# A third seven-product step in the last half of a macaron block's second down stages

## The reference, cut to what matters

```python
def swiglu(h, wg, wu, wd):
    return (jax.nn.silu(h @ wg) * (h @ wu)) @ wd
...
x = x + 0.5 * swiglu(rmsnorm(x, ffn1_norm[i]), ffn1_wg[i], ffn1_wu[i], ffn1_wd[i])
x = x + hybrid_mixer(rmsnorm(x, mix_norm[i]), ...)
x = x + 0.5 * swiglu(rmsnorm(x, ffn2_norm[i]), ffn2_wg[i], ffn2_wu[i], ffn2_wd[i])
return rmsnorm(x, final_norm)
```

## Time and profile before

| | |
|---|---|
| median of 3 runs | 1812.29 us (1810.42 to 1814.05) |
| profiled execution | 1811.32 us, span of its instructions 1809.5 us |
| TensorE matmul busy | 1796.6 us, 99% of the span, 8109 instructions |
| VectorE busy | 1555.6 us, 86% |
| ScalarE busy | 1069.5 us, 59% |
| DMA | 386.20 MB, mean 213 GB/s |

### The profile page before, as it was taken

The page is one execution under the profiler, slowest core; times in us unless marked ns, Lnnn a source line. Parts: engine busy times, 40 slices in busy tenths (PEclk is TensorE's granted clock), DMA queues, the critical chain, the costliest instruction groups (busy, mean ns, idle before and its releaser), DMA issues.

```text
span 1809.5 us, 22149 instructions
## 1 busy us (share of the span) xinstructions
PE 1796.6 (99%) x8109; PEld 1476.4 (82%) x8110; DVE 1555.6 (86%) x1913; ACT 1069.5 (59%) x1424; POOL 309.2 (17%) x514
## 2 busy tenths in 40 slices
PE   9999999999999999999999999999999999999998
PEld 7778888888888888888788888888888888888886
DVE  7989998889999997679567867899999879999997
ACT  6656655555666566556577745566665455666554
POOL 1122221002222100000122300122221000332100
PEclk9999999999999999999999999999999999999999
DMA  7778887678888667766544655678886677888764
GB/s 244 209 222 234 246 243 219 198 218 237 236 239 245 209 201 215 210 202 201 151 133 117 209 175 175 210 230 237 242 238 216 203 222 224 240 238 252 239 202 159
DMA packets 209661, 386.20 MB, mean 213 GB/s; under 512 B 20164, under 2 KB 25008, under 8 KB 209424
## 3 DMA queue, kind: packets, MB, share of 16 engines
q1 hardware_dynamic: 185008, 352.37, 62.5%
q0 software_dynamic: 22016, 30.90, 8.2%
q10 hardware_dynamic: 2528, 1.52, 0.3%
HBM read 368.98 MB, written 4.19 MB: 206 GB/s over the span
## 4 chain that ended last, share of the span: by engine, by line
PE 87%; DVE 7%; DMA 3%; ACT 1%; issue 1%; ACTq 0%; DVEq 0%; SPq 0%
PE ps L829 18%; PE ps L831 18%; PE ps L830 18%; PE ps L847 7%; PE ps L849 7%; PE ps L848 7%; PE ps L817 3%; PE ps L809 3%; PE ps L811 3%; DVE w_lo L1899 2%; DMA raw<-in_ffn_wg_dram 2%; PE ps L896 2%; DVE wt_lo L1971 1%; DMA w_lo<-in_ffn_wg_dram 1%; DVE wt L1961 1%
## 5 line engine op out<-in xcount | busy, mean ns | idle before, releaser
L1899 DVE TENSOR_TENSOR w_lo<-raw,w_hi 128x1024 fp32r<-128x1024 f32 (+1 forms) x565 | 645.0, 1159 | 108.5 <-ACT w_hi L1379 104.3
L1379 ACT ACTIVATE w_hi<-raw 128x1024 fp32r<-128x1024 f32 x565 | 587.9, 1054 | 203.5 <-PE ps L831 109.0
L829 PE MATMUL ps<-w_hi,hT_hi 128*128 128x512 f32 x972 | 381.7, 393 | 1.4 <-ACT gu L1473 1.2
L831 PE MATMUL ps<-w_hi,hT_lo 128*128 128x512 f32 x972 | 378.9, 390 | 0.0
L830 PE MATMUL ps<-w_lo,hT_hi 128*128 128x512 f32 x972 | 378.6, 390 | 0.0
L1430 ACT ACTIVATE wt_hi<-wt 128x1024 fp32r<-128x1024 f32 x180 | 189.7, 1054 | 289.4 <-DVE wt L1961 289.4
L737 POOL DMA_DIRECT2D gu_raw<-gu_sq x352 | 188.4, 544 | 362.4 <-DVE gu_sq L2146 352.5
L1971 DVE TENSOR_TENSOR wt_lo<-wt,wt_hi 128x1024 fp32r<-128x1024 f32 x180 | 219.3, 1218 | 0.0
L829 PEld LDWEIGHTS ps<-w_hi,hT_hi 128*128 128x128 f32 x972 | 182.6, 188 | 39.1 <-ACT gu L1473 1.6
L831 PEld LDWEIGHTS ps<-w_hi,hT_lo 128*128 128x128 f32 x972 | 182.4, 188 | 38.8
L830 PEld LDWEIGHTS ps<-w_lo,hT_hi 128*128 128x128 f32 x972 | 182.6, 188 | 36.6
(11 more groups left out here) (319 smaller groups left out, 2824.9 us busy)
## 6 DMA issues: line engine op xcount, KB each, us to landing
raw<-in_ffn_wu_dram SPq DMA_DIRECT2D x176, 512.0 KB, 5.0
raw<-in_ffn_wd_dram SPq DMA_DIRECT2D x176, 512.0 KB, 4.8
raw<-in_ffn_wg_dram SPq DMA_DIRECT2D x175, 512.0 KB, 4.7
raw<-in_w_in_dram SPq DMA_DIRECT2D x88, 512.0 KB, 3.7
w_lo<-in_ffn_wg_dram POOLq DMA_DIRECT2D x72, 256.0 KB, 6.7
raw<-in_w_out_dram SPq DMA_DIRECT2D x32, 512.0 KB, 4.2
gu_raw<-gu_sq POOLq DMA_DIRECT2D x352, 32.0 KB, 3.6
x_parked<-x SPq DMA_DIRECT2D x8, 256.0 KB, 5.3
```

Of the source, the lines that this page charges most:

```text
L829: mm(o, x_hi, w_hi[:, s, kk, :], start=begin, stop=False, skip_group_check=skip)
L831: ins = mm(o, x_lo, w_hi[:, s, kk, :], start=False, stop=last and kk == GK - 1, skip_group_check=skip)
L1379: act.activation(w_hi[:, c % SLOTS, :, :], raw[:, c % SLOTS, :, :], ACT.Copy).then_inc(hi_ready, 1)
L1899: tt(w_lo[:, s, 0:own, :], raw[:, s, 0:own, :], w_hi[:, s, 0:own, :].bitcast(F32), ALU.subtract).then_inc(lo_ready, 1)
```

## The change

The table of the second half gets a third seven-product step, for k-step 5. The steps follow each other with one plain slot between (before, two), and the first starts at slot 26 instead of 28. The plain slots are reordered to make room.

```diff
-         [(LEFT, 0), (LEFT, 2), (LEFT, 4), (LEFT, 5), (LEFT, 6), (LEFT, 7), (LEFT, 8), (LEFT, 9),
-          (PAIR, 1), (PAIR2, 1), (RIGHT, 0), (RIGHT, 2), (PAIR, 3), (PAIR2, 3)]
-         + [(RIGHT, q) for q in (4, 5, 6, 7, 8, 9)]]]
+         [(LEFT, 0), (LEFT, 2), (LEFT, 4), (LEFT, 6), (LEFT, 7), (LEFT, 8), (PAIR, 1), (PAIR2, 1), (LEFT, 9),
+          (PAIR, 3), (PAIR2, 3), (RIGHT, 0), (PAIR, 5), (PAIR2, 5)]
+         + [(RIGHT, q) for q in (2, 4, 6, 7, 8, 9)]]]
```

## The result

The kernel after takes 1816.33 us (median of 19 runs, 1814.13 to 1821.59), the kernel before beside it 1811.89 us (19 runs, 1809.39 to 1815.26): a ratio of 1.0023, with a 95% interval from 1.0017 to 1.0029, or 4.2 us more (3.1 to 5.3). The forecast was 3.2 us more.

What follows compares the result with a forecast made beforehand. TensorE, busy 99% of the span, was taken to bound the kernel. First FFN 2.96 + 0.22 + 0.3 − 0.68 = +2.8 us, second +0.4, together 3.2 on 1812.29: 1815.5 us, range 1812.4 to 1818.4.

Steps and rivals of the forecast that it cites:

- part 1: Second half of each FFN's down stage: C's 21 matmuls replace 24, saving 0.68 us per FFN.
- part 2: One plain slot between steps: VectorE's weight sums not fully hidden, 0.22 us lost at B, 0.3 at C.
- 0.30 + 3.82: Chain from one step's end to the next one's first remainders: 0.30 us to the first sum, 3.82 us more.
- A: The half's first seven-product step, k-step 1, moved from slots 28 and 29 to 26 and 27.
- part 3: First FFN: A's weight work queues ahead of x_operand, so TensorE waits 2.96 us (2.6 to 3.3) ahead of A.
- The three hand-overs: Hand-overs between engines in the chain ahead of A, 0.1 us each, giving the bounds 2.6 to 3.3 us.
- rival 3: First FFN: TensorE's clock falls behind the wait ahead of A, seven slow matmuls, +1.5 us, 1817.0 us; chance 0.06.
- the prediction's own sign for this rival: A granted clock below 1.00 behind TensorE's pause ahead of A.
- C: The added third seven-product step, k-step 5, at slots 32 and 33.
- rival 4: Load of C's second block (slot 33) comes late, 1.0 to 1.3 us per FFN, 1817.8 us; chance 0.12.
- part 4: Second FFN: no wait ahead of A, TensorE +0.15 us, adds to x 0.7 to 0.8 later, end +0.4 us.
- B: The half's second seven-product step, k-step 3, moved from slots 32 and 33 to 29 and 30.

Runs made afterwards that it cites:

- e7: Kernel after with the mixer's first-chunk transposes after slot 22 instead of 23 and x_operand after slot 25 instead of 27: 1813.47 us against 1812.22, ratio 1.0008.
- e4: Kernel after with no plain slot between A and B and two between B and C: 1819.66 us, one execution.
- e3: Kernel before with only the first seven-product step moved to slot 26, second still at 32, no third step: 1814.29 us against 1811.68, ratio 1.0022.
- e10: The kernel of e3 executed once more, unedited: 1813.90 us.
- e1: Kernel after repeated without edit: 1815.57 us against 1811.68 for the kernel before, ratio 1.0027.
- e12: Kernel after repeated without edit: 1817.20 us against 1811.15 for the kernel before, ratio 1.0026.
- e8: Kernel after repeated without edit, one execution: 1818.79 us.
- e9: Kernel after repeated without edit, one execution: 1816.28 us.

## Why the prediction was right, and which term was off

**Matmuls (part 1).** The saving of 0.68 us an FFN shows nowhere by itself, but the sums that hold it come out: e7's half, without a wait, is 0.2 us shorter than before's, and TensorE's half of the second FFN 0.16, where 0.68 less two covers gives 0.2 to 0.3.

**One plain slot as cover (part 2).** Predicted 0.22 and 0.3 us, bounds 0.2 to 0.6; measured 0.2 for each in the first FFN and 0.25 in the second. e4 bears out the sum 0.30 + 3.82 (2.9 us of wait by it, 2.8 measured).

**A ahead of `x_operand` (part 3).** Right in mechanism and nearly to the digit in its lengths: from A's first sum to ScalarE's part 5.29 us predicted and 5.27 measured, to VectorE's end 7.82 and 7.80, to A 8.01 and 8.01. The chain of 8.01 us holds within 0.02 us in the five profiles of the kernel after. That the times from the span's start agree as well (A at 672.60 predicted, 672.64 in the first profile) is chance: A's first sum lies anywhere from 661.37 to 664.71 in the five. The other end of the subtraction, TensorE at 669.64, was taken from one execution, in which VectorE had lost 1.17 us to a late block. The block stands in the earlier trace rows, as ScalarE's wait of 2.66 us at 652.36, but the prediction read from it only how long a load takes. That this execution had lost about as much as the five lose on average (0.9 us) is luck; read from one without a late block, the same sum would have given about 1.9 us. The five profiles give waits of 2.04, 2.43, 2.46, 2.89 and 3.84 us, 2.73 on average against 2.96; the bounds of 2.6 to 3.3 hold one of the five. The three hand-overs from which those bounds were made hardly vary; the loads do.

**The clock (rival 3).** This is the term that was mis-sized. Its price was right (predicted 1.5 us; 1.6, 1.4 and 1.7 measured), its chance of 0.06 was not: the clock fell in three of the five profiles, which was the prediction's own sign for this rival. The row that spoke against it showed 1.00 in a stretch behind the last matmul, one pause in one execution; e4 has two equal waits of 2.8 us with and without the fall, so one such row could not exclude it. It also was no alternative to the forecast but a cost that some executions add: 0.9 us on average of the five.

**Loads behind C (rival 4).** At C itself no load ended a wait. They were late a little further on, for the last slots of the half: ScalarE waited 2.02 us for a block at 1793.82 and VectorE 0.54 behind it. e3 and e10 have no C and a late block near the same place too (ScalarE waited 1.63 and 1.95 us), but there VectorE did not wait behind it.

**The second FFN (part 4).** TensorE's half: predicted +0.15, measured -0.16. The adds to x: predicted 0.7 later than before, measured 0.4 (1790.48 - 1786.88 less the 3.18 by which TensorE came later to slot 26). The end: predicted +0.4, measured +0.7 to 0.8. The late load, which the step left out, is the difference: in the five profiles the stretch behind the last matmul is 0.5 us longer than in before where VectorE waited at most 0.26 us for that block (e1, e12), and 0.8 to 0.9 longer where it waited 0.54 to 0.95 (after, e8, e9). That the lateness at the end goes with C close behind B is shown (e3, e10 and e4 against the others): C's weight work takes the room that VectorE had. Why the blocks come late is not shown; since they also do without C (e3, e10), C's sums freeing a buffer later cannot be all of it.

**The sum.** The first FFN's half is 3.56 us longer on average of the five profiles: 2.73 of wait, 0.9 of clock, and about -0.1 for covers less saving. With -0.16 from the second FFN and 0.7 from the end (the mean of the five) that is 4.1 us, and 4.2 (3.1 to 5.3) was measured. Predicted were 2.8 + 0.4 = 3.2. The forecast stood just inside the 3.6 us that it took for what can be told from no change, the result just outside. The clock's 0.9 us is nearly all that lies between: the wait came out 0.2 shorter than predicted and the rest some 0.2 longer.

## What to carry to other kernels

When a step moves ahead in a hand-written order, list for each in-order queue what it overtakes: here one piece of bank work, pushed back 3.8 us by the step's own weight sums, cost 2.7 us of waiting on average where the step saves 0.68. A wait that is the difference between two engines' arrivals should be given with the scatter of both, and loads that come late well ahead of the place belong to it. A pause on a TensorE that is otherwise never idle is priced twice, by its length and by the matmuls at half the clock that may follow it.

## What the runs showed of the hardware

The granted clock fell to 0.50 behind waits of 2.46, 2.73, 2.80, 2.89, 2.92, 3.84 and 4.07 us inside a stage in which TensorE was otherwise busy all the time, and stayed at 1.00 behind waits of 1.84, 1.95, 2.04, 2.42, 2.43 and 2.81 us: the two lists overlap. The stretches at half the clock held 7 to 9 matmuls, 1.4 to 1.7 us of extra time, and 13 with 2.8 us behind the longest wait. In e8 the fall came late: the first four matmuls behind the wait still followed each other by 0.23 to 0.31 us, and only from 673.73 on by 0.39 and then 0.43.
